# Sixteen modulation vectors computed as rows, constants loaded later, and the last 128 tokens' gates kept on chip

## What is computed

```python
sh1, sc1, g1, sh2, sc2, g2 = split(silu(c) @ w_mod + b_mod, 6)   # two vectors c: context, latent
h = rmsnorm(x, norm1_g) * (1 + sc1) + sh1
x = x + g1 * mixer(h)                 # projections, gated scans, pooling, two up-projections
h = rmsnorm(x, norm2_g) * (1 + sc2) + sh2
x = x + g2 * peer(h)                  # 8 heads pick 16 of 16384 experts each, for every token
y = rmsnorm(x, final_g)
# peer:  out[t] = sum over picked e of  gate[t, e] * gelu(h[t] . u_tab[e]) * v_tab[e]
```

## Time and profile before

| | us |
|---|---|
| median of three runs | 2444.54 (2435.21 to 2444.95) |
| the profiled execution | 2442.27 |
| its span, first to last instruction | 2440.5 |
| first matmul of the first product (`xp`, 0) | starts at 91.9 |
| second half of the u blocks, with gates | about 1155 to 1657 |
| values, PE | 1678.4 to 2397.7 |

### The profile page before, as it was taken

How to read it: one execution, slowest core, us unless ns; L and a number is a source line. 1 busy time by engine, 2 the same in 40 slices (tenths; PEclk the granted TensorE clock), 3 DMA queues, 4 the chain that set the end, 5 groups by cost and what they waited for, 6 DMA issues and landing times.

```text
span 2440.5 us, 36211 instructions
## 1 busy us (share of the span) xinstructions
PE 2298.3 (94%) x11820; PEld 1983.8 (81%) x11820; DVE 1679.2 (69%) x3204; ACT 819.4 (34%) x1037; POOL 973.9 (40%) x576
## 2 busy tenths in 40 slices
PE   8699998989999999998999999996999999999995
PEld 7689988989999888786888888885888888888883
DVE  2359996021399999201899889985777777777775
ACT  1345553121323222222544444442222222222221
POOL 0122222222122444443222222224666666776661
PEclk9799998999899999999999999998999999999997
DMA  8211212433321444444688778888999999999981
GB/s 322 69 57 61 61 48 78 165 104 121 129 62 61 144 140 142 138 138 137 219 305 309 294 297 311 310 302 263 283 282 280 280 280 281 281 280 281 283 267 69
DMA packets 265843, 484.07 MB, mean 198 GB/s; under 512 B 148144, under 2 KB 148528, under 8 KB 263856
## 3 DMA queue, kind: packets, MB, share of 16 engines
q1 hardware_dynamic: 209184, 279.21, 36.8%
q0 software_dynamic: 36864, 134.23, 15.9%
q10 hardware_dynamic: 19728, 69.74, 7.2%
HBM read 410.76 MB, written 72.36 MB: 198 GB/s over the span
## 4 chain that ended last, share of the span: by engine, by line
PE 34%; issue 31%; DVE 13%; POOL 11%; DMA 5%; ACT 3%; POOLq 1%; DVEq 1%; ACTq 1%; SPq 0%
PE P L576 14%; PE P L438 12%; POOL rows L399 6%; DMA rows<-in_u_tab,Eg 4%; POOL wLo L382 3%; PE P L460 3%; DVE gq L1029 3%; PE P L599 2%; PE P L447 1%; POOL Eg L393 1%; DVE ohA L1224 1%; DVE hdir L1043 1%; DVE gs L1033 1%; DVE gr L1030 1%; DVE ohB L1222 1%
## 5 line engine op out<-in xcount | busy, mean ns | idle before, releaser
L635 ACT ACTIVATE wHi<-raw 128x1024 fp32r<-128x1024 f32 (+1 forms) x332 | 348.2, 1049 | 1310.6 <-PE P L610 509.5
L382 POOL TENSOR_TENSOR wLo<-raw,wHi 128x1024 fp32r<-128x1024 f32 x192 | 466.8, 2431 | 429.7 <-ACT wHi L635 429.5
L1263 DVE TENSOR_TENSOR wfLo<-wf,wfHi 128x512 fp32r<-128x512 f32 x128 | 314.0, 2453 | 173.5 <-ACT wfHi L635 173.5
L610 PE MATMUL P<-wfHi,wHi 128*128 128x512 f32 x1024 | 402.5, 393 | 21.2 <-DVE wfLo L1263 21.2
L576 PE MATMUL P<-hHi,wHi 128*128 128x512 f32 x1024 | 412.4, 403 | 3.7 <-DVE wLo L1212 3.3
L376 POOL TENSOR_TENSOR wLo<-raw,wHi 128x1024 fp32r<-128x1024 f32 (+1 forms) x76 | 178.7, 2352 | 587.1 <-ACT wHi L635 587.1
L610 PE MATMUL P<-wfHi,wLo 128*128 128x512 f32 x1024 | 409.3, 400 | 0.0
L576 PE MATMUL P<-hHi,wLo 128*128 128x512 f32 x1024 | 405.5, 396 | 0.0
L576 PE MATMUL P<-hLo,wHi 128*128 128x512 f32 x1024 | 405.5, 396 | 0.0
L610 PE MATMUL P<-wfLo,wHi 128*128 128x512 f32 x1024 | 404.4, 395 | 0.0
L399 POOL DMA_INDIRECT rows<-in_u_tab,Eg x128 | 135.0, 1054 | 362.8 <-DVE rows L1205 341.7
(11 more groups left out here) (162 smaller groups left out, 3297.7 us busy)
## 6 DMA issues: line engine op xcount, KB each, us to landing
raw<-in_ublk SPq DMA_DIRECT2D x128, 512.0 KB, 3.7
raw<-in_v_tab SPq DMA_DIRECT2D x128, 512.0 KB, 3.8
raw<-in_wblk SPq DMA_DIRECT2D x116, 512.0 KB, 4.0
gel_scratch<-gel ACTq DMA_DIRECT2D x128, 256.0 KB
gate_scratch<-stage ACTq DMA_DIRECT2D x8, 4096.0 KB, 17.1
gsr<-gate_scratch SPq DMA_DIRECT2D x128, 256.0 KB
gsr<-gel_scratch SPq DMA_DIRECT2D x128, 256.0 KB
x<-in_xT SPq DMA_DIRECT2D x1, 2560.0 KB, 12.3
```

What stands on the lines that cost most here:

```text
L382: pool.tensor_tensor(wLo[:, j % 2, :], raw[:, j, :], wHi[:, j % 2, :].bitcast(f32), ALU.subtract).then_inc(raw_used[j], 1)
L610: last = nc.tensor.matmul(P[k // 2][:, k % 2, :], w_[:, j % 2, k * 128:(k + 1) * 128], x_[:, j % 2, :], start=(first and a == 0 and b == 0 ...
L635: return nc.scalar.activation(out, in_, f, **kw)
L1263: V.tensor_tensor(wfLo[:, j % 2, :], wf[:, j % 2, :], wfHi[:, j % 2, :].bitcast(f32), ALU.subtract).then_inc(s["wlo_ready"], 1)
```

## The change

Two separate edits. In the prologue, the first sixteen modulations are computed in pairs of blocks with the operands exchanged: the two columns of cvec are stationary and 256 columns of two blocks move, so that the result is two rows of 256 numbers in PSUM. Two DVE copies bring the rows to SBUF (`crow`, in the memory of `tb`), and sixteen PE transposes of a 2x128 piece put them where `mods(0, 16)` reads them; it now waits for `crow_tr`. The norm sum now stands after 4 of 8 pairs. ident is loaded first; the other five constants are issued after block 17 instead of block 11; the save of x is issued after ACT's `normed(0)` instead of ahead of the squares. In the expert stages, the gates of the last 128 latent tokens (t = 3) are no longer stored: SP waits for three stores of each half, loads gates for 384 tokens a block in 6 pieces, and DVE multiplies the last 128 tokens' gelus with `stage` directly, in a second instruction a block. The other edits renumber `raw_used`.

```diff
-    NSMALL = 6
+    NSMALL = 5
+    crow = tb[0:2, :, :].rearrange("p k t -> p (k t)")[:, 0:16 * 128]
@@ SP
+        sp_.dma_start(ident[:, :], ident_d).then_inc(s["c_ld"], 16)
-            if n == 12:
+            if n == 18:
                 for dst, src in ((invc[:, :, :], invc_d), (poolw[:, :, :], pw_d), (gw[:, :, :], gw_d),
-                                 (iota16[:, :], iota_d), (ident[:, :], ident_d), (iota128[:, :], iota128_d)):
+                                 (iota16[:, :], iota_d), (iota128[:, :], iota128_d)):
-            if n >= RAW:
-                sp_.wait_ge(raw_used[j], n // RAW)
+            if RAW <= n < 16 + RAW:
+                sp_.wait_ge(s["crow_mm"], (n - RAW) // 2 + 1)
+            elif n >= RAW:
+                sp_.wait_ge(raw_used[j], n // RAW - 4)
-            sp_.dma_start(gsr[:, j, 0, :].rearrange("p (c t) -> p c t", c=8),
-                          gate_out[:, :, ds(i * 4 + j, 1), :].rearrange("c p a t -> p c (a t)")
+            sp_.dma_start(gsr[:, j, 0, 0:TB - 128].rearrange("p (c t) -> p c t", c=6),
+                          gate_out[0:6, :, ds(i * 4 + j, 1), :].rearrange("c p a t -> p c (a t)")
-            sp_.wait_ge(gate_st[h], 16 * (NT - 1))
+            sp_.wait_ge(gate_st[h], 16 * (NT - 2))
@@ PE
+        def modulation_rows(r):
+            a = 2 * r % RAW
+            for j in (a, a + 1):
+                pe.wait_ge(raw_ld[j], r // 2 * 16 + 16)
+            for k in range(KC):
+                last = nc.tensor.matmul(P[r // 4][0:2, r // 2 % 2, r % 2 * 256:r % 2 * 256 + 256]
+                                        .rearrange("p (a n) -> p a n", a=2), cvec[:, 2 * k:2 * k + 2],
+                                        raw[:, a:a + 2, k * 128:(k + 1) * 128], start=(k == 0), stop=(k == KC - 1))
+            last.then_inc(s["crow_mm"], 1)
-        for m in range(8):
-            modulation(m)
+        for r in range(4):
+            modulation_rows(r)
         norm_sum(0)
-        for m in range(8, 16):
-            modulation(m)
+        for r in range(4, 8):
+            modulation_rows(r)
+        for half in range(2):
+            pe.wait_ge(s["crow_ready"], half + 1)
+            for m in range(8 * half, 8 * half + 8):
+                last = nc.tensor.transpose(P[3][:, 1, MODC + m * 2:MODC + m * 2 + 2], crow[:, m * 128:(m + 1) * 128],
+                                           ident[0:2, 0:2])
+        last.then_inc(s["crow_tr"], 1)
@@ ACT
-        act.wait_ge(s["c_ld"], 32)
+        act.wait_ge(s["c_ld"], 48)
-        act.dma_start(x_save, x[:, :, :]).then_inc(s["x_sv"], 16)
         squares(0)
         normed(0, scl1, 0)
+        act.dma_start(x_save, x[:, :, :]).then_inc(s["x_sv"], 16)
-        def gates_out(t, half):
-            if not isinstance(t, int):
+        def gates_out(t, half, kept=False):
+            if kept:
+                act.wait_ge(gate_st[half], t * 16)
+            elif not isinstance(t, int):
...
+            if kept:
+                return
             act.wait_ge(s["bank_free"], t * 32 + (half * 16 + 18))
             act.dma_start(gate_in[ds(t * 2 + half, 1), :, :].rearrange("a p m -> (a p) m"),
...
-        with act.Fori(1, 4) as t:
+        with act.Fori(1, 3) as t:
             gates_out(t, 0)
             gates_out(t, 1)
+        gates_out(3, 0, kept=True)
+        gates_out(3, 1, kept=True)
@@ DVE
         inv_rms(0)
+        for half in range(2):
+            dve.wait_ge(s["crow_mm"], 4 * half + 4)
+            V.tensor_copy(crow[:, half * 1024:(half + 1) * 1024].rearrange("p (b n) -> p b n", b=2), P[half][0:2, :, :]
+                          ).then_inc(s["crow_ready"], 1)
         mods(0, 16)
-                V.tensor_tensor(wf[:, j % 2, :], gsr[:, j, 0, :], gsr[:, j, 1, :], ALU.mult).then_inc(s["wf_ready"], 1)
+                V.tensor_tensor(wf[:, j % 2, 0:TB - 128], gsr[:, j, 0, 0:TB - 128], gsr[:, j, 1, 0:TB - 128], ALU.mult)
+                V.tensor_tensor(wf[:, j % 2, TB - 128:TB].rearrange("p (c t) -> p c t", c=2),
+                                stage[:, :, ds(i * 4 + j, 1), :].rearrange("p c a t -> p c (a t)"),
+                                gsr[:, j, 1, TB - 128:TB].rearrange("p (c t) -> p c t", c=2), ALU.mult
+                                ).then_inc(s["wf_ready"], 1)
+        dve.wait_ge(s["bank_free"], 2 + 2 * (NE // 2))
         expert_weights(0)
```

More of the change, by code:

```diff
@@ L267, in build @@
              "w_hi act_held eg_ready gel_free bank_free gmm_done oh_ready sm_ready tr2_done wf_ready "
-             "whi_ready wlo_ready mod_read").split()
+             "whi_ready wlo_ready crow_mm crow_ready crow_tr mod_read").split()
     gel_st = [sem(f"gel_st{j}") for j in range(2)]
@@ L283, in vcol @@
         return vecs[:, ds(j, n)]
-    NSMALL = 6
+    NSMALL = 5
     def used(eng, name, m):
         pos = POS[name, m]
-        eng.wait_ge(raw_used[pos % RAW], pos // RAW + 1)
+        eng.wait_ge(raw_used[pos % RAW], pos // RAW - 3)
     def evicted(eng, name, m):
@@ L334, in _ @@
             for j in range(RAW):
-                sp_.wait_ge(raw_used[j], i + B_U // RAW)
+                sp_.wait_ge(raw_used[j], i + B_U // RAW - 4)
                 sp_.dma_start(raw[:, j, :], ublk[ds(i * RAW + j, 1), :, :].rearrange("a p n -> (a p) n")
@@ L339, in value_block @@
         def value_block(i, j):
-            sp_.wait_ge(raw_used[j], i + B_V // RAW)
+            sp_.wait_ge(raw_used[j], i + B_V // RAW - 4)
             sp_.dma_start(raw[:, j, :], v_tab[ds(i * (RAW * 128) + j * 128, 128), :]).then_inc(raw_ld[j], 16)
@@ L569, in expert_scores @@
         def expert_scores(i, n0, j):
-            pe.wait_ge(raw_used[j], i + ((B_U + n0) // 4 + 1))
+            pe.wait_ge(raw_used[j], i + ((B_U + n0) // 4 - 3))
             pe.wait_ge(s["gel_free"], i * 4 + (n0 + j + 1))
@@ L603, in values @@
         def values(i, j, first=False, final=False):
-            pe.wait_ge(raw_used[j], i + (B_V // 4 + 1))
+            pe.wait_ge(raw_used[j], i + (B_V // 4 - 3))
             pe.wait_ge(s["wlo_ready"], i * 4 + (j + 1))
@@ L913, in mods @@
         def mods(m0, cnt):
-            used(dve, "mod", m0 + cnt - 1)
+            if m0:
+                used(dve, "mod", m0 + cnt - 1)
+            else:
+                dve.wait_ge(s["crow_tr"], 1)
             for g in range(2):
@@ L946, in _ @@
         V.tensor_tensor(x[:, :, TA:T], x[:, :, TA:T], hs[:, :, 0:TB], ALU.add).then_inc(s["x_ready"], 1)
-        dve.wait_ge(s["c_ld"], 32)
+        dve.wait_ge(s["c_ld"], 48)
         lam = vecs[:, V_LAM:V_LAM + 16]
```

## The result

The changed kernel took 2414.20 us in the median of four runs (2413.26 to 2416.34); four runs of the kernel before gave 2443.43. The ratio is 0.9888, with an interval of 0.9865 to 0.9912: 27 us or 1.1% faster (the two medians are 29 apart, inside this interval). The forecast was 2419 within 2410 to 2437. In the two profiled executions the span fell from 2440.5 to 2411.9.

A forecast was written before the change was run, and what follows sets the result against it. It took the kernel as bound by the prologue's chain through PE and PE's idle time before the values. 9.3 - 0.3 + 4.6 + 10.9 = 24.5 us off 2442.27 gave 2417.8 (2420.0 against the median); forecast 2419, range 2410 to 2437.

The forecast's parts named there:

- (a): Prologue modulations as rows: PE done at 61.7 instead of 71.08 us, 9.3 us gained; bounds 13.4 gain, 9.0 loss.
- The step that decides the sign: Prologue rows from pair 2: slow PE clock for 4.8 us, then fast; slow throughout would lose 9.0 us.
- the eight transposes: Prologue, after the second row copy: eight PE transposes at 0.221 us each follow it, 1.8 us.
- (b): Prologue transfers: later constants hidden; issuing the moved store of x on the path, 0.3 us lost.
- (c): Late u blocks: dropping the seventh gate store removes a long ACT step, 4.6 us gained, bounds 0 and 5.
- (d): Start of values: without the eighth gate store loads start earlier, DVE is late next; 10.9 us gained, bounds 5 and 12.
- (e): Value blocks: the split product adds 0.14 us of DVE a block, within 1.32 us idle time; cost 0.
- (f): Value loop: a quarter less gate-load traffic gains 0; unrolled ACT code may cost 0 to 2 us, taken as 0.
- the low clock in the rows: Rival, chance 0.14: PE's clock stays low in the prologue rows, which lose 9.3 us with the store's issue; total 2436.
- another wait at the values: Rival, chance 0.07: the gelu store or gathers end last where values begin; 5 us gained there, total 2424.
- POOL's collision: Rival, chance 0.04: in every value block the second product waits for POOL's subtraction; 156 us slower, 2574.
- the gain was not taken back: Denies a rival, chance 0.05: gain lost before PE's first product and at the values; total 2442.

The follow-up runs named there:

- e2: The kernel before with the gate part alone (two gate stores dropped, value product split), old prologue kept: 2424.83 us, ratio 0.9942.
- e1: The changed kernel with its gate part undone, so the new prologue rows alone: 2428.65 us, ratio 0.9955.
- e5: The changed kernel with the store of x issued ahead of the squares again, as in the kernel before: 2420.8 us, single run.
- e6: The changed kernel with the five constants issued ahead of block 12 again: 2413.34 us, single run.
- e3: The changed kernel with the seventh gate store issued again, nobody waiting for it before the program's end: span 2419.9 us, single run.
- e8: The changed kernel with seven more copies of the second product in every value block, written to an unread tile: 2484.4 us, single run.
- e11: The changed kernel with each gate store cut into four of 1024 KB, one after each of the next four u blocks, ACT's loop unrolled: 2395.75 us, ratio 0.9810.
- e4: The changed kernel with the eighth gate store issued again, waited for only at the program's end: span 2420.8 us, single run.

## Why the prediction was right

**(a) The rows: 10.5 instead of 9.0.** The step times were as read, 0.43 us slow and 0.21 fast. Pair 2 started at 24.75 (24.1 forecast), pair 3 ended at 34.1 (33.6), the norm sum at 43.0 (42.4), pair 5 at 50.0 (49.6), pair 6 started at 51.66 (51.4) and pair 7 ended at 58.7 (58.6). The step that decides the sign was the clock: rows at the slow clock for 4.8 us and fast from then on. Measured were 4.9 us, from 24.75 to 29.7. The term that was mis-sized is the eight transposes: 0.65 us, not 1.8; one of a 2x128 piece takes 0.08 us, and I had taken 0.221 from one of 128x128. Those 1.1 us and 0.3 of the moved store make up most of the difference. In this pair of profiles 8.6 of the 10.5 were left at the u blocks. The first product ran at the slow clock for 6.1 us (81.43 to 87.5) instead of 4.2, which accounts for 0.9. Such a difference comes without the edit too: from the first product to the first u block the kernel before took 691.9 us, but e2, with the same prologue, 693.3, and e1, with the new one, 693.3 as well.

**(b) The moved transfers: 0, as forecast,** by e5 and e6. The forecast's 0.3 us for the issue was too high: it lies beside ACT's work, 0.65 us from one step to the next with it and 0.64 without. The 4 to 10 us that I gave the early constants once the rows were known were wrong; the prediction's own 0 was not.

**(c) The seventh store: 5.0 where 4.6 was forecast,** by e3. The table shows 8.0 for this stretch. The other 3 us are shorter stalls behind the six stores that stayed. Runs with the same six stores differ by more (12.7 to 24.1 us in e1 to e8, the seventh store's step left out), so these 3 us can be chance alone; without them the span would have fallen by some 25, close to the forecast's 24.5. The sum had no term for these stalls and their scatter; it is the largest thing it left out, and it held 16 us, as e11 shows.

**(d) The eighth store: 11.0 at this place, 10.9 forecast.** The size was right and the reason half wrong: the prediction put it on SP's wait for the store, and e4 shows that the wait was 2.9 of it and the store's traffic beside the first loads 8.0. Dropping the store takes away both, so the size did not depend on which it was; had the store been kept and only the wait dropped, the same reasoning would have forecast 10.9 and got 2.9. DVE is late next, as said: PE's idle time of 10.24 ends with `wfLo`, the same in e2 and e11.

**(e), (f) The values: +0.07 us of DVE's time a block and no time on the path.** The forecast had 0.14: by the earlier trace rows and the rows after, the second product starts before the first has ended. The 0 to 2 us for ACT's unrolled code were a guess; no run shows such a cost, and e11, where the whole loop is unrolled, has ACT's steps at 7.38 us as before. PE's fast clock came a little sooner, at 1654.0 after a start at 1650.9, against 1683.3 after 1678.4: fewer slow matmuls, 0.7 us.

The rivals: the low clock in the rows is refuted by the spacing of 0.21 us from 12.37 on; another wait at the values by PE's releaser there; POOL's collision did not come at this size but is real (e8); and the gain was not taken back, by e1 and e2.

## What to carry to other kernels

A store of several MB in one instruction, issued by ACT here, delayed gathers that POOL had issued and loads that SP had issued; cut it and spread the pieces, and don't put it beside the first loads of the next stage, even if nobody waits for it. Where a matmul has a thin operand, try it as the stationary one, so that the many columns move, and look at the granted clock: here both forms cost the same at the same clock, and only one of them kept the fast one. Before trusting a cover, double the suspected work until it breaks: here it held 0.60 us and broke at 1.4.

## What the hardware showed that I had not expected

- One store of 4 MB cost mostly 2 to 5 us a time in a loop whose loads are small, another amount in each run, and 8.0 us beside a burst of loads. In pieces of 1 MB its cost is hardly to be seen (0.65 us in 24 pieces).
- PE busy without a gap at a granted clock of 0.50 for 18 us, with two columns moving; the same product with 256 columns moving reached 1.00.
- An overflow of 0.15 us on DVE cost 0.57 us a block in the mean, because DVE and POOL then hold each other up.
- The early rows: the profile's clock column reads full speed where the instructions are 0.43 us apart. In this view of the changed kernel (the stretch, busy time of PE, PEld, DVE, ACT and POOL, then the clock) it stands at 1.00, which the spacing of 0.21 us from 12.37 on does not allow for the first rows. The spacing is the better witness there.

```profile
8.00:12.00 4.00, 3.85 (x10) 1.19 (x11) 0.00 (x0) 0.00 (x0) 0.00 (x0) 1.00 1.06 451
```
